# Moving products of a gated recurrence to GpSimd, re-ordering a tap sum, and re-ordering the opening of a two-block model on one core

## The reference, cut to what matters

```python
shift, scale, gate = split(silu(c) @ mod_w[0] + mod_b[0], 3)      # also for c_ctx
hx = rmsnorm(x, norm_g[0]) * (1 + scale) + shift                   # also hc from ctx
va, vg, ga, xb, gb = split(hx @ w_in, 5)                           # 1024 channels each
y = layernorm(conv31(va * sigmoid(vg)) + b)                        # depthwise, 31 taps
y_a = silu(y) * silu(ga)
u = conv4(xb)                                                      # depthwise, 4 taps
# for two directions d (the second runs backwards), per head of 128 channels:
r, i = sigmoid(u @ w_r + b_r), sigmoid(u @ w_i + b_i)
a = exp(-8 * r * softplus(-lam))
b = sqrt(1 - a*a) * (i * u)                                        # i * u: the product that moves
h_t = a_t * h_(t-1) + b_t                                          # first over ctx, then over x
y_b = (h_forward + h_backward) * silu(gb)
out = x + gate * (concat(y_a, y_b) @ w_out)
```

## Time and profile before

| | |
|---|---|
| median of 3 runs | 3258.42 us (3257.64 to 3265.5) |
| the profiled execution, its own time | 3252.31 us |
| its span on the core | 3250.2 us |
| TensorE busy | 2983.3 us, 92% |
| VectorE busy | 1786.2 us, 55% |
| GpSimd busy | 1283.8 us, 40% |
| ScalarE busy | 1093.8 us, 34% |
| mean granted TensorE clock | 0.964 of full speed |

### The profile page before, as it was taken

How to read it: one execution, slowest core, us unless ns; L and a number is a source line. 1 busy time by engine, 2 the same in 40 slices (tenths; PEclk the granted TensorE clock), 3 DMA queues, 4 the chain that set the end, 5 groups by cost and what they waited for, 6 DMA issues and landing times.

```text
span 3250.2 us, 40045 instructions
## 1 busy us (share of the span) xinstructions
PE 2983.3 (92%) x13930; PEld 2301.9 (71%) x13930; DVE 1786.2 (55%) x2307; ACT 1093.8 (34%) x1431; POOL 1283.8 (40%) x1546
## 2 busy tenths in 40 slices
PE   5999999988999998989799999998999999998997
PEld 3787777756778786867688887776676666665775
DVE  6599999964354316453723222435456555556353
ACT  5334443423120000001332222223455556665332
POOL 2244444346734434436423323775211112111575
PEclk8999999989999999999899999999999999998999
DMA  7511122254311231113311012233222111221323
GB/s 286 161 62 62 56 73 68 69 187 149 116 30 52 75 116 39 49 35 124 107 35 33 26 39 96 93 89 125 59 46 46 39 41 46 47 40 40 131 81 112
DMA packets 113277, 258.55 MB, mean 80 GB/s; under 512 B 24608, under 2 KB 37984, under 8 KB 112368
## 3 DMA queue, kind: packets, MB, share of 16 engines
q1 hardware_dynamic: 83440, 189.43, 19.8%
q10 hardware_dynamic: 29696, 67.21, 5.7%
HBM read 223.97 MB, written 32.64 MB: 79 GB/s over the span
## 4 chain that ended last, share of the span: by engine, by line
PE 60%; DVE 19%; issue 9%; ACT 5%; POOL 4%; DMA 2%; DVEq 1%; POOLq 0%; ACTq 0%; SPq 0%
PE ps L627 16%; PE ps L628 15%; PE ps L629 15%; DVE ps L2063 5%; POOL t_wl L585 3%; PE ps L1171 2%; DVE t_tt L1996 2%; PE ps L1188 1%; POOL t_wh L580 1%; PE ps L985 1%; PE ps L987 1%; PE ps L986 1%; DVE t_pr L2522 1%; DVE t_ii L2074 1%; DVE t_pb L2281 1%
## 5 line engine op out<-in xcount | busy, mean ns | idle before, releaser
L627 PE MATMUL ps<-t_h_hi,t_wh 128*128 128x512 f32 x2464 | 1018.7, 413 | 82.7 <-POOLq L588 38.5
L580 POOL CAST t_wh<-t_wst 128x1024 fp32r<-128x1024 f32 (+2 forms) x306 | 328.1, 1072 | 1825.2 <-PE ps L629 1674.3
L628 PE MATMUL ps<-t_h_lo,t_wh 128*128 128x512 f32 x2464 | 986.5, 400 | 0.0
L629 PE MATMUL ps<-t_h_hi,t_wl 128*128 128x512 f32 x2464 | 985.0, 400 | 0.0
L585 POOL TENSOR_TENSOR t_wl<-t_wst,t_wh 128x256 fp32r<-128x256 f32 (+2 forms) x1224 | 949.4, 806 | 24.5
L627 PEld LDWEIGHTS ps<-t_h_hi,t_wh 128*128 128x128 f32 x2464 | 472.1, 192 | 237.2 <-issue 108.1
L628 PEld LDWEIGHTS ps<-t_h_lo,t_wh 128*128 128x128 f32 x2464 | 471.9, 192 | 113.3 <-issue 8.6
L629 PEld LDWEIGHTS ps<-t_h_hi,t_wl 128*128 128x128 f32 x2464 | 470.4, 191 | 114.6
L2063 DVE SCALAR_TENSOR_TENSOR ps<-t_upad,t_vec,ps 128x1024 f32<-128x1024 f32 x224 | 274.6, 1283 | 6.6 <-DVE ps L2057 0.9
L627 PE MATMUL ps<-t_y_hi,t_wh 128*128 128x512 f32 x512 | 208.1, 406 | 25.3 <-DVEq L264 14.6
L629 PE MATMUL ps<-t_y_hi,t_wl 128*128 128x512 f32 x512 | 206.3, 403 | 0.0
(11 more groups left out here) (348 smaller groups left out, 4255.2 us busy)
## 6 DMA issues: line engine op xcount, KB each, us to landing
t_wst<-w_even_in SPq DMA_DIRECT2D x40, 512.0 KB, 3.5
t_wst<-w_ple SPq DMA_DIRECT2D x64, 320.0 KB, 2.9
t_wst<-w_even_out SPq DMA_DIRECT2D x32, 512.0 KB, 3.6
t_wst<-w_fox_in SPq DMA_DIRECT2D x32, 512.0 KB, 3.6
t_modw<-w_mod SPq DMA_DIRECT2D x6, 2048.0 KB, 18.5
t_xr<-x_d ACTq DMA_DIRECT2D x6, 2048.0 KB, 11.5
t_wst<-w_gla_in SPq DMA_DIRECT2D x24, 512.0 KB, 3.8
t_wst<-w_odd_in_a SPq DMA_DIRECT2D x16, 512.0 KB, 3.6
```

The source lines that it names most:

```text
L580: pool.tensor_copy(wh[b][:, 0:w], wst[b][:, 0:w]).then_inc(S("w_high"), 1)
L627: pe.matmul(o, w1, x1, start=start and k == 0, stop=False)
L628: pe.matmul(o, w1, x2, start=False, stop=False)
L629: last = pe.matmul(o, w2, x1, start=False, stop=stop and k == kts - 1)
```

## The change

Three edits, all in the opening and the eight heads.

1. **The opening.** x comes in two transfers with a semaphore each. The context is queued before chunk 1 instead of before chunk 2. Chunks 4 and 5 wait for four used chunks instead of two and three. The sum of the context's squares moves on VectorE ahead of the scaling of x, and on TensorE its `stats` come right after those of x, ahead of chunk 1. ScalarE does both logarithms, then both exponentials, and all four `mod_row` after them.
2. **Head 0's taps.** A list `CONV_FIRST` puts 22 taps into slot 2 before the first one goes into slot 3; only the last eight go by turns. `q` and `drive` stand after taps 24 and 29.
3. **GpSimd.** `recurrence(h)` follows the split of tile 5 of each head: the low part of `yb` in four pieces of 256 columns (not in head 0), and `ii[d] * u` in four pieces of 320 columns for each direction. `times_u` and `low` go from VectorE. VectorE's `drive` waits for the products (`e_iu`), and so does ScalarE before it writes `xbp` and `u` of the next head.

```diff
+    CONV_FIRST = [(j, 0) for j in range(7)] + [(j, 0) for j in range(8, 23)] + [(7, 1)] + \
+        [(j, (j + 1) % 2) for j in range(23, TAPS)]
...
-        sp.dma_start(xr[:, :].rearrange("p (k t) -> p k t", k=KT),
-                     dram["xT"].rearrange("(k p) t -> p k t", p=P)).then_inc(S("x_loaded"), 16)
+        for q in range(2):
+            sp.dma_start(xr[:, 4 * q * T:4 * (q + 1) * T].rearrange("p (k t) -> p k t", k=4),
+                         dram["xT"][4 * q * P:4 * (q + 1) * P, :].rearrange("(k p) t -> p k t", p=P))\
+                .then_inc(S(("x_loaded", "x_more")[q]), 16)
...
-                sp.wait_ge(S("mod_used"), c - 2)
+                sp.wait_ge(S("mod_used"), NEARLY if c >= NEARLY else c - 2)
...
-            if c == 2:
+            if c == 1:
                 sp.dma_start(ctxr[:, :].rearrange("p (k t) -> p k t", k=KT),
...
+        def recurrence(h, first_head=False):
+            if not first_head:
+                pool.wait_ge(S("e_yh"), h)
+                for q in range(4):
+                    c = slice(q * T // 4, (q + 1) * T // 4)
+                    ins = pool.tensor_tensor(yb_lo[:, c], yb[:, c], yb_hi[:, c].bitcast(F32), ALU.subtract)
+                ins.then_inc(S("e_yl"), 1)
+            for d in range(2):
+                pool.wait_ge(S("e_evac"), 8 * h + 12 + 2 * d)
+                for q in range(4):
+                    c = slice(q * TC // 4, (q + 1) * TC // 4)
+                    ins = pool.tensor_tensor(ii[d][:, c], ii[d][:, c], u[:, c], ALU.mult)
+                ins.then_inc(S("e_iu"), 1)
...
         mod_chunk(0)
+        stats(0, sq0)
+        pe.wait_ge(S("sq_ready"), 2)
+        pe.matmul(bank(5, 0, C), ones, cx_rs[:, :], start=True, stop=True).then_inc(S("stats"), 1)
         mod_chunk(1)
         turn_chunk(0)
-        stats(0, sq0)
         turn_chunk(1)
         mod_chunk(2)
-        pe.wait_ge(S("sq_ready"), 2)
-        pe.matmul(bank(5, 0, C), ones, cx_rs[:, :], start=True, stop=True).then_inc(S("cx_stats"), 1)
         turn_chunk(2)
...
+                act.wait_ge(S("e_iu"), 2 * i + 2)
             A(xbp[:, XB0:XB0 + T], slot(0), ACT.Copy)
...
+            taps = CONV_FIRST if i is None else CONV
+            for n, (j, a) in enumerate(taps):
...
-        def times_u(h, i):
-            for d in range(2):
-                line.go(TT_(ii[d][:, :], ii[d][:, :], u[:, :], ALU.mult))
-        def low(h, i):
-            if i is not None:
-                dve.wait_ge(S("e_yh"), i + 1)
-                TT_(yb_lo[:, :], yb[:, :], yb_hi.bitcast(F32), ALU.subtract).then_inc(S("e_yl"), 1)
...
             for d in range(2):
+                dve.wait_ge(S("e_iu"), 2 * h + d + 1)
                 dve.wait_ge(S("e_sqrt"), 2 * h + d + 1)
...
-        LRU_AT = {7: times_u, 12: low, 18: q, 28: drive}
+        LRU_AT = {18: q, 28: drive}
...
-        even_head(None, LRU_AT)
+        even_head(None, {24: q, 29: drive})
```

More of the change, by code:

```diff
@@ L588, in split_tile @@
             pool.sem_inc(S("w_split"), 1)
-        for name, times, widths in STREAMS:
+        def recurrence(h, first_head=False):
[11 more added lines that the diff above has]
+                ins.then_inc(S("e_iu"), 1)
+        for name, times, widths in STREAMS:
+            if name == "w_even_in":
+                for j, w in enumerate(widths):
+                    split_tile(name, 0, j, w, widths, 0)
+                    if j % 6 == 5:
+                        recurrence(j // 6, j == 5)
+                with pool.Fori(0, times - 1) as i:
+                    for j, w in enumerate(widths):
+                        split_tile(name, i + 1, j, w, widths, 0)
+                        if j % 6 == 5:
+                            recurrence(2 * i + 2 + j // 6)
+                continue
             for half in range(passes(name)):
@@ L773, in even_head @@
             if opening:
-                pe.wait_ge(S("c_low"), 1)
+                pe.wait_ge(S("ctx_ready"), 2)
             else:
@@ L1357, in _ @@
         for k in range(KT):
-            act.wait_ge(S("x_loaded"), 16)
+            act.wait_ge(S(("x_loaded", "x_more")[k // 4]), 16)
             if k >= 2:
@@ L1361, in _ @@
             A(squares[:, (k % 2) * T:(k % 2 + 1) * T], col(xr, k), ACT.Square).then_inc(S("x_sq"), 1)
[L1362 to L1365, removed]
         act.wait_ge(S("ctx_loaded"), 16)
@@ L1368, in _ @@
             A(squares[:, (2 + k) * T:(2 + k) * T + C], ctxr[:, k * C:(k + 1) * C], ACT.Square).then_inc(S("c_sq"), 1)
[L1369 to L1372, removed]
+        act.wait_ge(S("stats"), 1)
+        line.go(A(sq0[:, :], slot(3), ACT.Ln, bias=eps6[:, 0:1], scale=1.0 / D))
+        act.wait_ge(S("stats"), 2)
+        line.go(A(cx_rs[:, :], bank(5, 0, C), ACT.Ln, bias=eps6[:, 0:1], scale=1.0 / D))
+        line.sync(1)
+        A(sq0[:, :], sq0[:, :], ACT.Exp, scale=-0.5).then_inc(S("rs"), 1)
+        line.sync()
+        A(cx_rs[:, :], cx_rs[:, :], ACT.Exp, scale=-0.5).then_inc(S("rs"), 1)
+        for c in range(NEARLY):
+            mod_row(c)
         for k in range(KT + 1):
@@ L1378, in _ @@
                 if k == 0:
-                    act.wait_ge(S("c_scaled"), 1)
+                    act.wait_ge(S("ctx_ready"), 1)
                 c = ctxr[:, k * C:(k + 1) * C]
@@ L1929, in _ @@
         dve.sem_inc(S("sq_ready"), 1)
+        dve.wait_ge(S("c_sq"), 8)
+        line(TT_(cx_rs[:, :], squares[:, 2 * T:2 * T + C], squares[:, 3 * T:3 * T + C], ALU.add))
+        for k in range(2, KT):
+            line(TT_(cx_rs[:, :], cx_rs[:, :], squares[:, (2 + k) * T:(2 + k) * T + C], ALU.add))
+        dve.sem_inc(S("sq_ready"), 1)
         dve.wait_ge(S("rs"), 1)
@@ L1934, in _ @@
             line.go(TT_(col(xr, k), col(xr, k), sq0[:, :], ALU.mult))
[L1935 to L1941, removed]
+        dve.wait_ge(S("rs"), 2)
         c3 = ctxr[:, :].rearrange("p (k c) -> p k c", c=C)
         line(TT_(c3, c3, cx_rs[:, :].rearrange("p (o c) -> p o c", o=1).to_broadcast((P, KT, C)), ALU.mult))
-        dve.sem_inc(S("c_scaled"), 1)
+        dve.sem_inc(S("ctx_ready"), 1)
         mv = modv[:, :].rearrange("p (l m v) -> p l v m", l=2, v=2)
@@ L1977, in _ @@
         dve.wait_ge(S("c_high"), 8)
-        TT_(hc_lo[:, :], ctxr[:, :], hc_hi[:, :].bitcast(F32), ALU.subtract).then_inc(S("c_low"), 1)
+        TT_(hc_lo[:, :], ctxr[:, :], hc_hi[:, :].bitcast(F32), ALU.subtract).then_inc(S("ctx_ready"), 1)
         dve.wait_ge(S("h_ready"), KT)
-        dve.wait_ge(S("c_low"), 1)
+        dve.wait_ge(S("ctx_ready"), 2)
         end(dve)
@@ L2043, in even_head @@
             acc, begun, last = [slot(2), slot(3)], [False, False], 0
-            for n, (j, a) in enumerate(CONV):
+            taps = CONV_FIRST if i is None else CONV
+            for n, (j, a) in enumerate(taps):
                 s, w = upad[:, j:j + T], V("conv_w", 8 * j + h)
@@ L2060, in even_head @@
                     o = acc[a]
-                    if a == 0 and all(b for _, b in CONV[n + 1:]):
+                    if a == 0 and all(b for _, b in taps[n + 1:]):
                         o, s = u_out, by_half(s)
@@ L2104, in last_low @@
             dve.wait_ge(S("e_yh"), 8)
+            dve.wait_ge(S("e_yl"), 7)
             TT_(col(h_lo, 7), yb[:, :], col(h_hi, 7).bitcast(F32), ALU.subtract).then_inc(S("e_yl"), 1)
-        even_head(None, LRU_AT)
-        line.repeat(6, 6 + 4 + 1 + 1 + TAPS + 4, lambda i: even_head(i, LRU_AT))
-        even_head(6, {7: times_u, 12: low, 18: q, 23: last_result, 26: last_low})
+        even_head(None, {24: q, 29: drive})
+        line.repeat(6, 6 + 4 + 1 + 1 + TAPS + 2, lambda i: even_head(i, LRU_AT))
+        even_head(6, {18: q, 23: last_result, 26: last_low})
         end(dve)
```

## The result

The changed kernel takes 3224.95 us (3224.16 to 3226.24, four runs) against 3259.71 us before in the same call: a ratio of 0.9891, 95% interval 0.9874 to 0.9908, so 35 us faster. Measured a second time beside other kernels it took 3228.29 against 3260.86 (0.9899, 0.9882 to 0.9916). The forecast was 3230.5 in a range of 3223 to 3243. Its profiled execution took 3224.75 us, span 3222.5, which is 27.7 under the profile before: the difference of the profiles is what I had summed (27.9), the difference of the medians is 7 us more. Both have to be explained.

The account below looks back on a forecast made before the run. VectorE was taken to bound the heads, with TensorE close behind at 66.34 us a head. Heads and tail 27.2 plus opening 0.7 gave 27.9 us, so 3258.4 - 27.9 = 3230.5 us, range 3223 to 3243.

Parts of the forecast that it names:

- The bound changes hands: Heads: VectorE falls from 69.4 to 64.6 us a head, so TensorE, needing 66.34, becomes the bound; 3.1 us less a head.
- VectorE's slack of 1.7 us a head: Heads: of the 4.8 us a head taken off VectorE, 1.7 us is left as slack behind TensorE.
- Seven heads and the tail: Head 7's taps start 23.4 us earlier, and head 7 itself, ended by VectorE, is 3.8 us shorter; 27.2 us together.
- (b): Distance from head 0's end to VectorE's start on head 7; the forecast had head 7's taps start 23.4 us earlier.
- (c): Distance from VectorE's start on head 7 to the end of its taps; the forecast had head 7 3.8 us shorter.
- GpSimd: Heads: `recurrence` costs GpSimd 9.8 us at the low end, which was taken, or 16.4 us at the high end.
- the room: Heads: the next head's tile 0 split ends at 24.7 and TensorE needs it at 29.5, leaving 4.8 us.
- the rival on the other side: Heads: GpSimd becomes the bound; no change, about 3255 us, chance 0.04, or slower, chance 0.03.
- Its limit: Heads: TensorE waits once `recurrence` and the split together take 18.5 us; 0.3% slower from some 25 us.
- Head 0's taps: Head 0: its taps end about 14 us earlier, but this is worth 0 us to the end.
- The opening: Before the heads: first use of the modulation comes between 0 and 4 us earlier; 0.7 us was taken.
- the rival of a fuller opening: Opening: TensorE is granted the upper clock level and VectorE's end decides, 4 us earlier; 3227 us, chance 0.12.

Follow-up runs that it names:

- more22: The changed kernel with 22 extra small GpSimd products (result unread) behind `recurrence` in each head; 3300.02 us, ratio 1.0126 to the kernel before.
- more9: The changed kernel with nine extra small GpSimd products (result unread) behind `recurrence` in each head; 3242.72 us, ratio 0.9950 to the kernel before.
- no_taps: The changed kernel with the second edit (head 0's tap list) taken back; 3227.01 us against 3257.18 for the kernel before.
- tiles_before2: The changed kernel with the first two weight tiles queued ahead of modulation chunk 2 instead of behind chunk 3; 3227.13 us against 3260.86 for the kernel before.
- tiles_before3: The changed kernel with the first two weight tiles queued between modulation chunks 2 and 3; 3227.43 us against 3260.86 for the kernel before.
- gps_only: The kernel before with the third edit alone (products and low part on GpSimd); 3231.43 us against 3257.18, ratio 0.9918.
- open_only: The kernel before with the first edit alone (the opening); 3254.43 us against 3257.18, ratio 0.9981.

## Why the prediction was right, point by point

**The bound changes hands.** Right. Heads of 66.3 us were forecast from head 1 of the trace before; they are 66.27. TensorE has no idle row between 154 and 613 us, neither for gb nor for a split. VectorE's slack of 1.7 us a head was forecast, and shows as waits of 3 us at `u_hi` and 0.3 at tile 2; the rest comes from operations that got shorter as their GpSimd neighbour moved away (the two results 1.23 us each instead of 1.57 and 1.65, conv4 5.35 instead of 6.04).

**Seven heads and the tail.** 23.4 + 3.8 us were forecast, 24.5 + 3.9 measured ((b) and (c)). The missing 1.1 us: I let VectorE's results keep the 1.6 us that they took beside a split, and so put head 7's start 0.8 us after tile 2. With results of 1.23 us VectorE is ready 0.3 us before tile 2 ends, and starts at its end. The other 0.4 us are six heads of 66.27 instead of 66.34.

**GpSimd.** 9.8 us were forecast for `recurrence`, 9.1 measured; the room was forecast as 4.8 us and was 5.4. The price of the rival on the other side was right in kind: more22 is slower than before. Its limit was also placed well (18.5 us for `recurrence` and split together; more9 has 20.5 and waits 2.17). What I missed, and missed again in the expectation of more9, is that this room is not free of VectorE: the second half of it lies beside `q`.

**Head 0's taps.** 0 forecast, 0 measured beside the third edit (no_taps). In the kernel before they are worth 5 us of (b). I had written that this edit by itself is worth nothing to the end; that step looked only at when TensorE wants VectorE, which is enough where TensorE is the bound and not where VectorE is. The forecast did not use it.

**The opening** is the term that was mis-sized: 0.7 us forecast, 3.2 measured in the profile at the end of head 0. The modulation came 6.5 us earlier in the profile, because the context's sum took 3.1 us instead of 4.9 (in the kernel before it had run beside the first split), because TensorE had the upper level for its last chunk (1.93 us) and the last turns (1.05 instead of 1.87) and in part for chunk 1 (2.78), and because VectorE, which ended at 44.2 and not 48.5, did not hold it up. I had this as the rival of a fuller opening, at 4 us with 0.12. So 3.2 of the 6.5 us reached the end of head 0. Of the rest, 2.2 us went in the making of h (20.0 us instead of 17.8), where the splits of tiles 0 and 1 now run beside it; tiles_before2 and tiles_before3 show that this is so. Another 1.4 us went later in head 0: TensorE was granted the lower level for one of the late pieces of the modulation, whose 16 matmuls took 2.79 us at 119.70, where they had taken 1.50 at 124.22 before.

**The 7 us between profiles and medians.** The openings in the table answer most of this. Five profiles with the old opening end head 0 at 153.2, 153.8, 155.5, 157.6 and 157.8, mean 155.6. The profile before was the fastest of them. In it TensorE was granted the upper level for chunk 1 (1.92 us); in gps_only, with the same order, it was not:

```profile
25.45 3.64 PE L735 MATMUL ps<-t_modw,t_silp 128*32 128x512 f32 x16 [1.21 <-DMA t_modw<-w_mod]
```

Seven profiles of the new opening with the tiles last give 148.6 to 153.3, mean 150.7. So the opening is worth 4.9 us on average, not 3.2. This mean carries the scatter of a few profiles, and open_only's times put the opening at 3 to 6 us. Behind the heads, from the end of the taps to the first tile of the pooling mixer, the profile before took 200.8 us and the change 203.1; the others with either code lie from 199 to 206. To the end of the span it is 2578.0 and 2581.9 us, the other twelve from 2575.3 to 2587.3. So the profile before was quick in both stretches, by 2.4 us in the opening and 3.9 behind the heads, which is as much as it lay under its median (6.1 us). 24.5 + 3.9 + 4.9 = 33.3 us, against 34.8 and 32.6 measured. My conversion from profile to median (the profile was 6.1 us under the median, and I assumed the changed one would be too) failed for that reason: the changed kernel's profile lay on its median. That my sum of 27.9 met the profiles' 27.7 was luck: it was 5.4 us too small, and the pair of profiles happened to show 5.6 us too little, 1.7 in the opening and 3.9 behind the heads. In medians the forecast was 5.5 us too high (3230.5 against 3224.95). The cause of the quick stretch behind the heads stays open.

## What to carry to other kernels

When the bounding engine is relieved, look for the next one's own period first, in a stretch of the old trace where it is not held: here one undisturbed head gave 66.3 us to within 0.1, and capped a saving of 4.8 us a head at 3.1. Work moved to GpSimd was cheap here beside VectorE operations with one SBUF input (a split's four pieces 2.85 us) and dear beside those with two (5.17 us), so its room must be read together with what VectorE does in it; work that is pushed along by the move counts too. A profile of one execution can be several us off its kernel's median; a distance between two events in the repeated part (here good to 0.1 us) settles what medians cannot.

## What the runs showed of the hardware that was not expected

A GpSimd copy of 1024 columns, 1.04 us beside taps, took 5.29 us beside VectorE's back-to-back scaling of x and of the context with two SBUF inputs, and the scaling went on at its usual pitch of 1.15 us an operation: there VectorE lost nothing, as `q` lost nothing beside the single products of more22. In more9, with four pieces of a split beside `q`, both lost (5.17 for 2.85, 4.03 for 2.88), and so they did in tiles_before2 (6.58 for 2.8, 12.24 for 9.17). What decides who pays, no run here shows.

```profile
39.77 5.29 POOL L585 CAST t_wh<-t_wst 128x1024 fp32r<-128x1024 f32 x1 [37.76 <-DMA t_wst<-w_even_in]
```

The opening's order of TensorE work being fixed, the level granted for single chunks still differed from profile to profile (1.92 or 3.64 us for chunk 1 with the old order), and the end of head 0 by up to 4.6 us.
